# One gelu pass on ScalarE for the dense tokens of the U stage, and larger row budgets there

## What is computed

```
q = hf @ wq                                    # per head: two halves of 128
v1, i1 = top_k(q1 @ k1.T, 16); v2, i2 = top_k(q2 @ k2.T, 16)
cs, ci = top_k(v1[:, None] + v2[None, :], 16)  # 16 of 256 candidates per head
e = i1[ci // 16] * 128 + i2[ci % 16]           # 8 heads x 16 = 128 experts of 16384 per token
g = softmax(cs)
act = gelu(einsum('tkd,td->tk', u_tab[e], hb)) # jax.nn.gelu: the tanh form
out = einsum('tk,tkd->td', g * act, v_tab[e])  # D = 2048
y = rmsnorm(x + out, final_g)
```

## Time and profile before

| | us |
|---|---|
| runs | 4665.11, 4674.65, 4679.74 |
| span of the profiled execution | 4667.9 |
| PE busy | 4588.6 (98%) |
| DVE busy | 2713.5 (58%) |
| ACT busy | 539.6 (12%) |
| POOL busy | 956.5 (20%) |
| U stage, blocks 0 to 61 | 2778.3 to 3206.6 |
| U stage, blocks 62 to 127 | 3206.6 to 3749.4 |
| V stage with the last norm | 3750.7 to 4667.9 |

### The profile page before, as it was taken

One profiled execution on the slowest core, in us unless ns is written; L12 is line 12 of the kernel. 1 busy time (PEld: TensorE's weight loads), 2 busy tenths in 40 slices (PEclk: granted clock), 3 DMA queues, 4 the chain that ended last, 5 costly groups with the idle time before them and its releaser, 6 DMA issues.

```text
span 4667.9 us, 50792 instructions
## 1 busy us (share of the span) xinstructions
PE 4588.6 (98%) x20474; PEld 3719.0 (80%) x20474; DVE 2713.5 (58%) x4679; ACT 539.6 (12%) x1229; POOL 956.5 (20%) x691
## 2 busy tenths in 40 slices
PE   8999999999999999999999999999999999999998
PEld 7888888888767676667776678888888888888887
DVE  4434500017678686745556658886788855556552
ACT  1111200000111111010000111112222200000000
POOL 1000000000112313014443332222332323222220
PEclk9999999999999999999999999999999999999999
DMA  4434444545669779659999888888999999999994
GB/s 174 139 133 140 172 147 155 176 172 178 219 237 334 290 266 350 221 211 361 362 370 377 332 327 327 329 332 323 346 356 345 348 380 410 395 413 420 421 417 164
DMA packets 264157, 1350.34 MB, mean 289 GB/s; under 512 B 45729, under 2 KB 52129, under 8 KB 140338
## 3 DMA queue, kind: packets, MB, share of 16 engines
q1 hardware_dynamic: 170066, 663.90, 38.9%
q0 software_dynamic: 93856, 683.19, 37.0%
HBM read 1306.30 MB, written 40.16 MB: 288 GB/s over the span
## 4 chain that ended last, share of the span: by engine, by line
PE 87%; DMA 8%; DVE 3%; issue 1%; ACT 0%; POOL 0%; DVEq 0%; POOLq 0%; ACTq 0%
PE ps L404 39%; PE ps L738 16%; PE ps L758 9%; PE pm L758 9%; PE ps L563 4%; DMA RA<-in_uT 4%; PE ps L625 2%; DMA RA<-in_peer_v 2%; DMA RING<-in_peer_u,table 2%; PE ps L518 1%; PE pm L511 1%; PE pm L467 1%; PE ps L571 1%; DVE BIG L1252 1%; DMA BIG<-in_peer_v,table 1%
## 5 line engine op out<-in xcount | busy, mean ns | idle before, releaser
L404 PE MATMUL ps<-X,BIG 128*128 128x320 f32 (+1 forms) x5632 | 1394.9, 409 | 7.5 <-DVE X L1444 4.2
L404 PEld LDWEIGHTS ps<-X,BIG 128*128 128x128 f32 x5632 | 1068.4, 190 | 317.6 <-issue 10.0
L738 PE MATMUL ps<-X,RA 128*128 128x256 f32 x4096 | 902.2, 380 | 20.9 <-DMA RA<-in_uT 20.7
L738 PEld LDWEIGHTS ps<-X,RA 128*128 128x128 f32 x4096 | 772.6, 190 | 131.6 <-DMA RA<-in_uT 22.6
L974 DVE SCALAR_TENSOR_TENSOR CUR<-RING,wexp,CUR 128x2048 f32<-128x2048 f32 x288 | 676.8, 2350 | 258.0 <-DMA RING<-in_peer_v,table 150.3
L966 DVE CUSTOM_DVE_ANT_0 RING<-RING,CUR 128x2048 f32<-128x2048 f32 x286 | 652.0, 2289 | 280.0 <-DMA RING<-in_peer_u,table 146.9
L2044 POOL DMA_INDIRECT RING<-in_peer_u,table x222 | 352.3, 1587 | 951.1 <-DVE hidden L966 644.0
L2044 POOL DMA_INDIRECT RING<-in_peer_v,table x224 | 332.1, 1483 | 920.1 <-DVE CUR L974 746.5
L404 PE MATMUL ps<-BIG 128*128 128x256 f32 (+1 forms) x2048 | 504.4, 408 | 7.9 <-DVE BIG L1430 5.6
L404 PEld LDWEIGHTS ps<-BIG 128*128 128x128 f32 x2048 | 389.9, 191 | 117.8 <-DVE BIG L1430 7.0
L758 PE MATMUL ps<-BIG,RA 128*128 128x256 f32 x2048 | 465.4, 380 | 8.7 <-DMA RA<-in_peer_v 8.7
(11 more groups left out here) (317 smaller groups left out, 3082.5 us busy)
## 6 DMA issues: line engine op xcount, KB each, us to landing
BIG<-in_w_in_b SPq DMA_DIRECT2D x128, 1024.0 KB, 5.8
RA<-in_uT SPq DMA_DIRECT2D x256, 512.0 KB
RA<-in_peer_v SPq DMA_DIRECT2D x256, 512.0 KB
BIG<-in_w_gb_b SPq DMA_DIRECT2D x32, 1024.0 KB, 5.1
BIG<-in_w_ga_b SPq DMA_DIRECT2D x32, 1024.0 KB, 4.9
BIG<-in_w_gla_o_b SPq DMA_DIRECT2D x32, 1024.0 KB, 5.0
BIG<-in_w_mix_b SPq DMA_DIRECT2D x32, 1024.0 KB, 6.7
BIG<-in_w_q_b SPq DMA_DIRECT2D x32, 1024.0 KB, 8.1
```

The lines of the kernel that those rows point to most:

```text
L404: last = pe.matmul(bank[:, 0:n], w(k, j * P, P), src[:, k, 0:n], start=(k == 0), stop=(k == kt - 1))
L738: last = pe.matmul(bank[:, 0:ND], half_slot[slot_of[m]][:, k % 8, :], h2T[1][:, k, 0:ND], start=(k == 0), stop=(k == KT - 1))
```

## The change

ACT does the gelu of a block in one instruction (`Gelu_apprx_tanh`) that reads PSUM and writes `H`, or from block 64 on in two: the finished tokens' part goes to `u_work`, the rest to `H`. Both of DVE's steps of it are gone, the argument and the product, and so are the signals `sq_u`, `tanh_u` and `arg_u`. The PSUM bank is free after ACT. DVE keeps the product with the gates (before line 1522, now 1511) and waits for ACT only there and in `gate_tokens`. ACT's `serve` moves from the head of a block to behind its gelu. The factor 0.5 is now applied only to the softmax weights of the gathered tokens. The budgets of rows per block go from 2.8 to 3.4, or 4.3 once all routing is done (`ROUTED`), in blocks 0 to 61, and from 4.2 to 5.0 (`U_PACE`) in blocks 62 to 124.

```diff
+U_PACE = 5.0
+ROUTED = 4 * PH + PH // 2
...
-                step(dve.tensor_scalar(gsum[g][0:n, 0:heads], gsum[g][0:n, 0:heads], 0.5, None, ALU.mult))
+                if g == 0 or t == 2:
+                    step(dve.tensor_scalar(gsum[g][0:n, 0:heads], gsum[g][0:n, 0:heads], 0.5, None, ALU.mult))
...
             def gate_tokens(q, n):
                 dve.wait_ge(*ps_done.at("g", q))
                 dve.wait_ge(*g_copied.at(q))
-                dve.wait_ge(*h_ready.at(n - 1))
+                dve.wait_ge(*gelu_u.at(n - 1))
...
             for b in range(NB):                                   # DVE
-                scratch = H[:, b, :] if b <= G_AT else u_work
-                bank = banks.of("u", b)
                 if b > G_AT:
                     gate_tokens(b - 1 - G_AT, b)
-                dve.wait_ge(*sq_u.at(b))
-                arg_u.on(dve.scalar_tensor_tensor(out=scratch, in0=scratch, scalar=1.0, in1=bank[:, 0:ND], op0=ALU.add,
-                                                  op1=ALU.mult), b)
                 spare((b, "u"), 0.0)
                 if b < G_AT - 1:
                     paced(work_1, 3.9)
-                    paced(work, 2.8)
+                    paced(work, 4.3 if routed.n == ROUTED else 3.4)
                 elif b < NB - 2:
                     onehots(b + 1 - G_AT)
-                dve.wait_ge(*tanh_u.at(b))
-                done = 4 * max(b - G_AT, 0)
-                if done:
-                    dve_step.on(dve.scalar_tensor_tensor(out=scratch[:, 0:done], in0=scratch[:, 0:done], scalar=1.0,
-                                                         in1=bank[:, 0:done], op0=ALU.add, op1=ALU.mult))
-                if done < ND:
-                    ins = dve.scalar_tensor_tensor(out=H[:, b, done:], in0=scratch[:, done:], scalar=1.0,
-                                                   in1=bank[:, done:ND], op0=ALU.add, op1=ALU.mult)
...
-                    ins = dve.tensor_tensor(H[:, b, 0:done], scratch[:, 0:done], H[:, b, 0:done], ALU.mult)
-                h_ready.on(ins, b)
-                banks.free(h_ready, "u", b)
+                if b > G_AT:
+                    done = 4 * (b - G_AT)
+                    dve.wait_ge(*gelu_u.at(b))
+                    dve.wait_ge(*g_copied.at(b - 1 - G_AT))
+                    h_ready.on(dve.tensor_tensor(H[:, b, 0:done], u_work[:, 0:done], H[:, b, 0:done], ALU.mult), b)
                 if G_AT - 1 <= b < NB - 3:
-                    paced(work, 4.2)
+                    paced(work, U_PACE)
...
             for b in range(NB):                                   # ACT
-                serve((b, "u"))
...
-                if b > G_AT:
-                    act.wait_ge(*h_ready.at(b - 1))
...
-                sq_u.on(fn(scratch, banks.of("u", b)[:, 0:ND], ACT.Square, scale=float(np.sqrt(0.044715))), b)
+                if done:
+                    act.wait_ge(*(h_ready.at(b - 1) if b > G_AT + 1 else row_used.at(last_row[0])))
+                    ins = fn(u_work[:, 0:done], bank[:, 0:done], ACT.Gelu_apprx_tanh)
+                if done < ND:
+                    ins = fn(H[:, b, done:], bank[:, done:ND], ACT.Gelu_apprx_tanh)
+                gelu_u.on(ins, b)
+                banks.free(gelu_u, "u", b)
...
-                act.wait_ge(*arg_u.at(b))
-                tanh_u.on(fn(scratch, scratch, ACT.Tanh, scale=float(np.sqrt(2.0 / np.pi))), b)
+                serve((b, "u"))
```

More of the change, by code:

```diff
@@ L301, in trunk @@
          mean_ready, sqln_ready, sd_root, affined, tanhed, gateB_ready, gateA_ready, ss2_done, rms2_ready, h2T_ready,
-         qp_ready, sc_ready, exps_done, gelu_tanh, root_g, sq_u, tanh_u, selT_ready, oh_scaled, ss3_done, root3,
+         qp_ready, sc_ready, exps_done, gelu_tanh, root_g, gelu_u, selT_ready, oh_scaled, ss3_done, root3,
          rows_kept, ones_made) = (
@@ L308, in trunk @@
                 "tanhed", "gateB_ready", "gateA_ready", "ss2_done", "rms2_ready", "h2T_ready", "qp_ready", "sc_ready",
-                "exps_done", "gelu_tanh", "root_g", "sq_u", "tanh_u", "selT_ready", "oh_scaled", "ss3_done", "root3",
+                "exps_done", "gelu_tanh", "root_g", "gelu_u", "selT_ready", "oh_scaled", "ss3_done", "root3",
                 "rows_kept", "ones_made"))
@@ L314, in trunk @@
          sd_ready, lned, silu_ready, mergedB_ready, part_ready, merged_ready, resid_ready, ms2_ready, h2_ready,
-         routed, shifted, gates_ready, row_used, gelu_arg, ss_g, y_g, arg_u, h_ready, onehot_ready, gm_ready,
+         routed, shifted, gates_ready, row_used, gelu_arg, ss_g, y_g, h_ready, onehot_ready, gm_ready,
          sum_ready, ms3_ready, y_ready, sums_ready) = (
@@ L321, in trunk @@
                 "part_ready", "merged_ready", "resid_ready", "ms2_ready", "h2_ready", "routed", "shifted",
-                "gates_ready", "row_used", "gelu_arg", "ss_g", "y_g", "arg_u", "h_ready", "onehot_ready", "gm_ready",
+                "gates_ready", "row_used", "gelu_arg", "ss_g", "y_g", "h_ready", "onehot_ready", "gm_ready",
                 "sum_ready", "ms3_ready", "y_ready", "sums_ready"))
@@ L1508, in _ @@
                 assert b != H_FOURTH - 1 or row_used.n >= FOUR_ROWS
-                dve.wait_ge(*tanh_u.at(b))
-                done = 4 * max(b - G_AT, 0)
-                if done:
-                    dve_step.on(dve.scalar_tensor_tensor(out=scratch[:, 0:done], in0=scratch[:, 0:done], scalar=1.0,
-                                                         in1=bank[:, 0:done], op0=ALU.add, op1=ALU.mult))
-                if done < ND:
-                    ins = dve.scalar_tensor_tensor(out=H[:, b, done:], in0=scratch[:, done:], scalar=1.0,
-                                                   in1=bank[:, done:ND], op0=ALU.add, op1=ALU.mult)
-                if 0 < done < ND:
-                    dve_step.on(ins)
-                if done:
+                if b > G_AT:
+                    done = 4 * (b - G_AT)
+                    dve.wait_ge(*gelu_u.at(b))
                     dve.wait_ge(*g_copied.at(b - 1 - G_AT))
-                    dve.wait_ge(*dve_step.now())
-                    ins = dve.tensor_tensor(H[:, b, 0:done], scratch[:, 0:done], H[:, b, 0:done], ALU.mult)
-                h_ready.on(ins, b)
-                banks.free(h_ready, "u", b)
+                    h_ready.on(dve.tensor_tensor(H[:, b, 0:done], u_work[:, 0:done], H[:, b, 0:done], ALU.mult), b)
                 if G_AT - 1 <= b < NB - 3:
-                    paced(work, 4.2)
+                    paced(work, U_PACE)
             for b in range(NB):
@@ L1903, in _ @@
             for b in range(NB):
-                serve((b, "u"))
-                scratch = H[:, b, :] if b <= G_AT else u_work
+                done = 4 * max(b - G_AT, 0)
+                bank = banks.of("u", b)
                 act.wait_ge(*ps_done.at("u", b))
-                if b > G_AT:
-                    act.wait_ge(*h_ready.at(b - 1))
                 if b == H_FOURTH:
                     act.wait_ge(*row_used.at(FOUR_ROWS - 1))
-                sq_u.on(fn(scratch, banks.of("u", b)[:, 0:ND], ACT.Square, scale=float(np.sqrt(0.044715))), b)
+                if done:
[5 more added lines that the diff above has]
+                banks.free(gelu_u, "u", b)
                 if b > G_AT:
```

## The result

The kernel after took 4686.13 us (median of 9 runs, 4681.35 to 4696.33), the one before 4673.34 on the same chip (9 runs, 4665.11 to 4679.74). By the medians it is 12.8 us slower, 0.27%. So the change is a small loss, at the edge of the 0.3% that counts as a change here, though its interval leaves 1 out. The forecast was 4679, some 4 us slower.

What follows compares the result with a forecast made beforehand. TensorE, busy 98%, bounds the kernel, with about 31 us of waits winnable. First part 0, second part +6, ScalarE 0, V stage -2 make +4 us on the median 4674.65: 4679 us, range 4655 to 4706.

Steps and rivals of the forecast that it cites:

- The limit changed hands: Second part: the limit passes from uT transfers (20.7 us) to VectorE, waiting for rows and late with one-hot matrices.
- the 3770 that was to show the turn wrong: Sign: V stage beginning after 3770 means the turn was wrong; 3745 to 3765 means the forecast is right.
- The first part: Blocks 0 to 61: added rows finish by 3218, just in time; cost 0, up to 10 us at a slower rate.
- Tables: ScalarE: three more pairs of table loads around the softmax's exps, none around tanhs; 7.7 us, zero on the path.
- the second part: Blocks 62 to 127, the deciding term: VectorE waits for rows and brings one-hot matrices late; +6 us.
- the ring's turn: Second part: time until a row slot is filled and used again in the three-slot ring, taken as 9.6 us.
- the prediction's own formula: Second part: a two-row block lasts (2.2 + 9.6 + 2.2 + 1.8)/2 = 7.9 us, three rows 11.8, one row 7.8.
- the slower rival: Second part: more rows lengthen the ring's turn, deciding from 10.0 us, past +14; +32 at 10.6, +60 at 11.4; chance 0.26.
- The V stage: V stage: rows end 168 us earlier, which buys nothing; change of tile moves off most waits; -2 us (-9 to +3).
- What the gelu gave back goes to rows: VectorE: time freed by the gelu is spent on added rows, 48 and 47 us, nearly one for one.
- the faster rival: Second part: uT waits go and VectorE keeps pace; with V -9 to -31 us, middle -20, 4655; chance 0.22.
- Turns by packet: Queues' packets average 3.9 and 7.3 KB; in V, halves get 149 of 419 GB/s: 3.5 us each, needed every 3.9.

Runs made afterwards that it cites:

- the two without: The gelu-alone kernel with the eight 256 KB pieces of x loaded beside V blocks 112 to 126, at second-part budgets 4.2 and 3.8: 4641.94 and 4648.08 us.
- the gelu alone: The changed kernel with both row budgets as before (2.8 and 4.2), so only the gelu moved to ScalarE: 4648.51 us, ratio 0.9941 to the kernel before.
- work put back: The gelu-alone kernel with 0.9 us of useless multiplications added on VectorE in blocks 64 to 125: 4669.64 us, ratio 1.0005 to the kernel before.
- the times at 4.6: The changed kernel with the row budget of blocks 62 to 124 at 4.6 instead of 5.0: 4673.59 us, ratio 1.0008 to the kernel before.
- the budgets alone: The kernel before with the new row budgets (3.4 or 4.3, and 5.0) and the old gelu on two engines: 4722.81 us, ratio 1.01.

## Why the prediction was right, and where not

**What it had right.** The time lies in its range, and the place and kind of the loss are the ones it named. The limit changed hands: waits for uT fell (7.9 us left; 5 had been let stand), waits for one-hot matrices came, and the two did not add. V began at 3765.3, at the far end of the 3745 to 3765 that it gave; but this execution was 3.0 us ahead when the U stage began, so like for like it is 3768, between that range and the 3770 that was to show the turn wrong. The first part cost nothing (428.96 and 428.87), with rows at a higher rate. VectorE did not fall short at the first matrices. The last row was issued at 4403 and used by 4428, for 4400 forecast, and VectorE then waited 225 us for the last blocks, so that 4160 to 4560 ran at 324 GB/s and no faster. Tables: the trace shows one load at the start of the stage and a pair around each of the three exps, and none beside the eight tanhs that stand between gelus. The Trainium skill, "ScalarE: Activation LUTs", section "Table sets: the hidden batching unit", says of its gelu set that it is separate from gelu_apprx_tanh, the function used here, and names no set that has it. By this trace it shares a set with tanh and not with exp. The gelu takes 384 ns in one piece, the lower end of the estimate:

```profile
L1900 ACT ACTIVATE BIG<-ps 128x256 f32<-128x256 f32 x62 | 23.8, 384 | 393.9 <-PE ps L740 393.9
L1900 ACT ACT_TABLE_LOAD x4 | 5.1, 1283 | 0.1
L1555 ACT ACT_TABLE_LOAD x3 | 3.8, 1283 | 0.1
```

**The term that was mis-sized: the second part.** It was to grow by 6 us and grew by 17.7, and in the terms of the sum the ring's turn was taken too short. I took 9.6 us. The 38 row transfers that stand in the chain of waits from 3207 to 3765 take 9.09 us in the mean, and with the 0.73 us until POOL issues the next, 9.8. By the prediction's own formula that is 8.0 us for a block of two rows and 12.0 for one of three: 54 x 8.0 + 6 x 12.0 + 3 x 7.8 = 527.4 instead of 520.8. That is 7 of the 11 us that are missing: from the end of block 62 to V the forecast had 521 + 17 + 5 = 543, and measured were 554.4 (3210.9 to 3765.3). VectorE's gates themselves show where the rest went. From the first to the last they take 534.6 us instead of 520.8, TensorE's waits included, of which 5 us had been let stand beside it. The 52 intervals with two rows are 8.30 us in the mean, where 7.9 was forecast (+21 us), the six with three 11.56 for 11.8 (-1), and the three with one 5.83 for 7.8 (-6), because VectorE catches up there. So a block of two rows costs more than even the measured turn gives, and what makes the last 0.3 us of it is open. There was no term for the clock, 6.8 us. The turn stayed just below the 10.0 from which the slower rival was to decide.

**The V stage.** I took -2 and it was +1.9, within its bounds (-9 to +3). The move of the change of tile away from the pieces of x did not pay; waits for peer_v went from 8.7 to 10.1. The pieces themselves do cost something: ahead of 4150 TensorE waits 6.4 to 16.8 us for peer_v in the ten profiles with the pieces there, and 2.5 and 2.2 in the two without. V and norm gained 8.8 us by it in the profile, which the times of whole runs do not resolve.

**The step that failed without being seen in the sum.** "What the gelu gave back goes to rows" was right as an account of VectorE's time and wrong as an account of worth: it led me to set the removed work at nothing. By itself it is worth 23 us by the medians, more than all the waits for uT that I held winnable at all. The premise was that an instruction of VectorE is worth what TensorE waits for VectorE, which was 1.3 us. But VectorE governs when rows are issued. In blocks of two rows it stood 8.38 apart against TensorE's 7.8, so it fell behind, and the transfers that its rows release fell otherwise beside the next halves of uT, at times four beside one half. I had that number and those transfers in one paragraph, and used them only as an argument against the faster rival. Then the rows' cost was too small to the same degree: not +6 from a base of 0, but +35 from a base of -23. That the sum came out near is in good part luck: two errors of opposite sign.

**Turns by packet.** They were to keep the waits on uT from growing, and the waits did not grow with 20 rows more. But the argument fails. That the halves had 149 of 419 GB/s in the V stage shows nothing of turns: TensorE uses a half of 512 KB in 3.46 us there, which is 151 GB/s, so they got what was asked for. And the number and order of rows is the same in the kernel before, in that with the gelu alone and in that with work put back, and the waits for uT are 20.7, 4.7 and 15.6 us. The share of the halves over a long stretch says nothing of one half beside four rows.

**What stays open.** That rows beside a half delay it is seen in their counts and times, and not followed packet by packet. Whether the rows' cost starts with the third row in a block, and why the times at 4.6 are as high as they are, is not settled.

## What to carry to other kernels

Price work on an engine off the critical path also by what it releases: time taken off VectorE was worth 23 us, 16 of which stood in the profile as waits for a transfer from another queue, and useless work in its place brought most of them back. When a change frees an engine and fills it again, run the two halves apart before judging either; here the first was -23 us and the rows after block 62 some +35. Where stages are compared by one profile each, find out first how far the same stage moves between two executions; here it was 5 us. Filler work of long transfers wants a stage where the consumer has slack and an end that comes before the last consumer: moved too early it makes matrices late, moved too late it makes the norm wait.

## What the runs showed of the hardware

- In the U and V stages of all twelve profiles 15 of 28 waits of TensorE of 2 to 3 us, and all 11 longer ones, came with a stretch at 1.2 GHz that began within the wait or up to 1.5 us behind it, most of them 3.4 us long. Such stretches cost 6.8 us in the second part after and 13.7 with the budgets alone; the wait of 14.9 us came with 13.7 us at half clock.
- One core moved 413 and 428 GB/s over two stretches of some us, with gathered rows and plain loads together, and 419 over 400 us.
- Gelu in its tanh form costs ScalarE what a square does, 384 ns for 128x256 out of PSUM, with no table load between it and a tanh, and one (1283 ns) each way between it and an exp.
- A transfer of one row for 128 partitions (1.05 MB) took 9.04 us from issue to landing in the mean of blocks 64 to 124 after, and 8.54 with the gelu alone.
